# VectorE's order in the FFN down products: the fourth block sum behind two adds, the third sum beside the first, the last norm's tiles interleaved

## The reference, cut to what matters

```python
def conv_ffn(xn, w_up, conv_w, conv_b, w_down):      # w_up 1024 x 5632, w_down 2816 x 1024
    u = xn @ w_up
    up = jnp.pad(u, ((0, 0), (CONV_WIDTH - 1, 0), (0, 0)))
    c = conv_b
    for j in range(CONV_WIDTH):
        c = c + conv_w[j] * up[:, j:j + s]
    val, gate = jnp.split(c, 2, axis=-1)
    return (jax.nn.silu(gate) * val) @ w_down

for layer in range(2):
    h = h + merge_heads(heads) @ w_out[layer]
    h = h + conv_ffn(rmsnorm(h, norm_ffn[layer]), w_up[layer], ...)
return rmsnorm(h, norm_final)
```

## Time and profile before

| what | us |
|---|---|
| median of 3 runs | 1731.66 (1730.42 to 1731.68) |
| the profiled execution: its time | 1731.79 |
| the profiled execution: its span from first to last instruction | 1730.0 |
| TensorE busy | 1701.5 (98% of the span) |
| VectorE busy | 1082.1 (63%) |
| GpSimd busy | 838.4 (48%) |
| ScalarE busy | 757.4 (44%) |

### The profile page before, as it was taken

The page is one execution under the profiler, slowest core; times in us unless marked ns, Lnnn a source line. Parts: engine busy times, 40 slices in busy tenths (PEclk is TensorE's granted clock), DMA queues, the critical chain, the costliest instruction groups (busy, mean ns, idle before and its releaser), DMA issues.

```text
span 1730.0 us, 25076 instructions
## 1 busy us (share of the span) xinstructions
PE 1701.5 (98%) x9544; PEld 1379.8 (80%) x9548; DVE 1082.1 (63%) x2221; ACT 757.4 (44%) x1606; POOL 838.4 (48%) x784
## 2 busy tenths in 40 slices
PE   9999999999999999999999999999999999999997
PEld 7886787787689877779878878787777988788785
DVE  6997734785653356525684684757775368568477
ACT  4626523213433344424444444446663364345345
POOL 8525456552357734335535535266443554453440
PEclk9999999999999999999999999999999999999998
DMA  6321323131233311124225224132112241441521
GB/s 186 109 81 54 112 63 119 53 108 37 80 102 119 107 53 49 55 69 117 79 73 146 73 77 131 52 131 98 49 50 73 74 135 49 122 122 49 155 64 49
DMA packets 174600, 152.46 MB, mean 88 GB/s; under 512 B 5720, under 2 KB 149464, under 8 KB 174480
## 3 DMA queue, kind: packets, MB, share of 16 engines
q1 hardware_dynamic: 172304, 148.32, 27.9%
q10 hardware_dynamic: 2176, 2.53, 0.4%
HBM read 147.65 MB, written 2.14 MB: 87 GB/s over the span
## 4 chain that ended last, share of the span: by engine, by line
PE 83%; DVE 13%; ACT 3%; issue 1%; DVEq 0%; ACTq 0%
PE ps L490 66%; DVE ffn_cv L2890 2%; PE ps L2425 2%; PE ps L2460 2%; PE ps L2445 2%; DVE h L2742 2%; DVE w_lo L341 2%; DVE ffn_cv L2904 1%; PE ps L1892 1%; DVE ffn_a_lo L2911 1%; PE ps L561 1%; PE ps L1870 1%; PE ps L2433 1%; DVE w_chain L320 1%; PE ps L1807 1%
## 5 line engine op out<-in xcount | busy, mean ns | idle before, releaser
L490 PE MATMUL ps<-x_hi,w_hi 128*128 128x512 f32 (+2 forms) x1432 | 532.3, 372 | 0.5 <-DVE x_lo L762 0.4
L490 PE MATMUL ps<-x_hi,w_lo 128*128 128x512 f32 (+2 forms) x1432 | 522.6, 365 | 0.0
L490 PE MATMUL ps<-x_lo,w_hi 128*128 128x512 f32 (+2 forms) x1432 | 522.2, 365 | 0.0
L223 POOL TENSOR_SCALAR w_hi<-w_raw 128x512 fp32r<-128x512 f32 x272 | 167.8, 643 | 501.2 <-PE ps L490 501.2
L227 POOL TENSOR_TENSOR w_lo<-w_raw,w_hi 128x512 fp32r<-128x512 f32 x272 | 360.1, 1354 | 5.9
L195 POOL TENSOR_TENSOR w_lo<-w_raw,w_hi 128x512 fp32r<-128x512 f32 x174 | 232.9, 1372 | 267.8 <-ACT w_hi L186 235.4
L490 PEld LDWEIGHTS ps<-x_hi,w_hi 128*128 128x128 f32 (+1 forms) x1432 | 269.4, 188 | 60.0 <-issue 16.5
L490 PEld LDWEIGHTS ps<-x_hi,w_lo 128*128 128x128 f32 (+1 forms) x1432 | 269.3, 188 | 44.0
L490 PEld LDWEIGHTS ps<-x_lo,w_hi 128*128 128x128 f32 (+1 forms) x1432 | 269.7, 188 | 40.3
L2890 DVE SCALAR_TENSOR_TENSOR ffn_cv<-ps,col,ffn_cv 128x510 f32<-128x510 f32 (+1 forms) x176 | 131.8, 749 | 150.8 <-ACT ffn_cv L2836 146.2
L490 PE MATMUL ps<-w_hi,ffn_a_hi 128*128 128x512 f32 x308 | 122.7, 398 | 10.7 <-DVE h L2742 10.0
(11 more groups left out here) (396 smaller groups left out, 2873.2 us busy)
## 6 DMA issues: line engine op xcount, KB each, us to landing
w_raw<-w_up SPq DMA_DIRECT2D x88, 512.0 KB, 5.0
w_raw<-od_w_in SPq DMA_DIRECT2D x12, 1024.0 KB, 5.3
w_raw<-w_in_fox SPq DMA_DIRECT2D x10, 1024.0 KB, 5.4
w_raw<-w_in_dil SPq DMA_DIRECT2D x10, 1024.0 KB, 5.3
w_raw<-w_out SPq DMA_DIRECT2D x8, 1024.0 KB, 5.0
w_raw<-w_down SPq DMA_DIRECT2D x8, 1024.0 KB, 5.0
w_raw<-ev_w_in SPq DMA_DIRECT2D x6, 1024.0 KB, 5.4
w_third<-w_down SPq DMA_DIRECT2D x18, 256.0 KB, 5.2
```

The source lines that it names most:

```text
L223: ins = pool.tensor_scalar(hi[:, c:min(c + PIECE, size)], raw[:, c:min(c + PIECE, size)], 1.0, 1.0, ALU.mult, ALU.mult)
L490: mm = pe.matmul(o, l, r, start=start and i == 0, stop=stop and i == 2, skip_group_check=again)
```

## The change

Five edits, all in the order of instructions; none is added or removed but the semaphore counts that follow from the order.

1. `early`: the fourth sum moves from behind the low of 6 to behind X6 t1, just ahead of the low of 4.
2. `early`: X6 t0 is taken ahead of Z t1.
3. `ConvFFN.vector`: the third sum moves from behind the low of unit n-2 to directly behind the first sum, ahead of the conv of unit n-2.
4. The four takes of X7 and X7b become a function `sevens`, called at the same place as before, but in layer 1's last part from within `Final.vector`.
5. `Final`: VectorE's and ScalarE's instructions go tile by tile interleaved instead of tile behind tile.

```diff
-            READS = ("X1", "X1", "Y5", "Y5", "Z", "Z", "X6", "X6", "X7", "X7b", "X7", "X7b", "Y3", "Y3", "W", "W")
+            READS = ("X1", "X1", "Y5", "Y5", "Z", "X6", "Z", "X6", "X7", "X7b", "X7", "X7b", "Y3", "Y3", "W", "W")
@@ early
                 g.low(dve, "6")
-                g.fourth_sum(dve)
                 g.low(dve, "7")
                 self.take(dve, "Y5", 0, "5")
                 self.take(dve, "Y5", 1, "5")
                 self.take(dve, "Z", 0, "2")
+                self.take(dve, "X6", 0, "6")
                 self.take(dve, "Z", 1, "2")
-                self.take(dve, "X6", 0, "6")
                 g.low(dve, "3")
                 self.take(dve, "X6", 1, "6")
+                g.fourth_sum(dve)
                 g.low(dve, "4")
+
+            def sevens(self, dve):
+
                 for t in range(2):
                     self.take(dve, "X7", t, "7")
                     self.take(dve, "X7b", t, "7")
@@ ConvFFN.vector
                         if u == u0 + n - 2:
                             self.down[part].group.first_sum(dve)
+                            self.down[part].group.third_sum(dve)
                         conv(u)
                         gate(u)
                         a11, a21 = cv[:, u % 4, 0, 0:2 * P], cv[:, u % 4, 0, 2 * P:S]
                         low(u, 1, 0, 1, a11).then_inc(self.first_ready.s, 1)
                         if u == u0 + n - 2:
-                            self.down[part].group.third_sum(dve)
                             self.down[part].group.second_sum(dve)
...
                     d.early(dve)
+                    if part < len(PARTS) - 1 or self.layer == 0:
+                        d.sevens(dve)
@@ Final.scalar
+                for tile in range(T):
+                    first(tile)
+                for tile in range(2):
+                    root(tile)
+                    scaled(tile)
+                for tile in range(2, T):
+                    root(tile)
+                for tile in range(2, T):
+                    scaled(tile)
@@ Final.vector
+                dve.wait_ge(self.gain_in, 16)
+                first(0)
+                first(1)
+                self.out.sevens(dve)
+                first(2)
+                add(0)
+                first(3)
+                inverse(0)
+                add(1)
+                last(0)
+                inverse(1)
+                last(1)
+                add(2)
+                add(3)
+                inverse(2)
+                last(2)
+                inverse(3)
+                last(3)
```

More of the change, by code:

```diff
@@ L2671, in __init__, with taken @@
                 self.summed, self.read = tally("down_summed", 7), tally("down_read", 16)
-                self.added = self.Added(self.read)
+                self.added = self.Added(self)
+            def taken(self, what, t):
+                return self.read.at([i for i, r in enumerate(self.READS) if r == what][t] + 1)
             def sums(self, pe, m, c, t, js, start):
@@ L2706, in last_half @@
                 for t in range(2):
-                    pe.wait_ge(self.read.s, self.read.at(1 + t))
+                    pe.wait_ge(self.read.s, self.taken("X1", t))
                     self.sums(pe, "6", "X", t, every, False)
@@ L2710, in last_half @@
                 for t in range(2):
-                    pe.wait_ge(self.read.s, self.read.at(7 + t))
+                    pe.wait_ge(self.read.s, self.taken("X6", t))
                     self.sums(pe, "7", "X", t, every, False)
@@ L2717, in last_tile @@
                     pe.wait_ge(W.lo_by_dve, g.lows + 3)
-                    pe.wait_ge(self.read.s, self.read.at(3 + t))
+                    pe.wait_ge(self.read.s, self.taken("Y5", t))
                     self.sums(pe, "3", "Y", t, range(g.kk), False)
@@ L2737, in take @@
                 r, c = self.TARGET[what]
-                before = {"Z": 1, "X7b": 3, "Y3": 7, "W": 9}.get(what)
+                before = {"Z": "X1", "X7b": "Y5", "Y3": "X6", "W": "X7"}.get(what)
                 if before:
-                    dve.wait_ge(self.read.s, self.read.at(before + t * (2 if what == "W" else 1)))
+                    dve.wait_ge(self.read.s, self.taken(before, t))
                 hv = h[:, 2 * r + t, 512 * c:512 * c + 512]
@@ L2812, in up @@
                     d = self.down[part - 1]
-                    taken = {d.bank["X"]: 12, d.bank["Y"]: 14, d.bank["Z"]: 6, d.bank["W"]: 16}
-                    pe.wait_ge(d.read.s, d.read.at(taken[self.up_bank(u, 0)]))
+                    last = {d.bank[what[0]]: what for what in ("X7b", "Y3", "Z", "W")}
+                    pe.wait_ge(d.read.s, d.taken(last[self.up_bank(u, 0)], 1))
                 for half in range(2):
@@ L2977, in scalar, with first @@
                 link(act.activation(seam_stat[:, 0, 0:1], eps_col[:, 0:1], ACT.Sqrt))
-                for tile in range(T):
+                def first(tile):
                     act.wait_ge(self.out.added.s, self.out.added.at(tile + 1))
@@ L2981, in scalar, with root @@
                                    accum_out=seam_stat[:, 0, tile:tile + 1]).then_inc(self.first_summed, 1)
-                for tile in range(T):
+                def root(tile):
                     act.wait_ge(self.out.added.s, self.out.added.at(4 + tile + 1))
@@ L2988, in scalar, with scaled @@
                                    bias=self.first[:, tile:tile + 1]).then_inc(self.rooted.s, 1)
+                def scaled(tile):
                     act.wait_ge(self.inverted.s, self.inverted.at(tile + 1))
@@ L2993, in scalar, with first @@
                     act.dma_start(out[0, tile * P:(tile + 1) * P, self.early(tile)], self.res[:, tile, self.early(tile)]).then_inc(self.stored, 16)
+                for tile in range(T):
[7 more added lines that the diff above has]
+                    scaled(tile)
             def vector(self, dve):
-                dve.wait_ge(self.gain_in, 16)
-                for tile in range(T):
+                def first(tile):
                     e = self.early(tile)
@@ L3002, in vector, with inverse, last @@
                                       ALU.add).then_inc(self.first_made, 1)
-                for tile in range(T):
-                    e = self.late(tile)
-                    self.out.add(dve, 1, tile)
+                def inverse(tile):
                     dve.wait_ge(self.rooted.s, self.rooted.at(tile + 1))
                     dve.reciprocal(seam_stat[:, 2, tile:tile + 1], seam_stat[:, 1, tile:tile + 1]).then_inc(self.inverted.s, 1)
+                def last(tile):
+                    e = self.late(tile)
                     dve.wait_ge(self.inverted.s, self.inverted.at(tile + 1))
@@ L3010, in vector, with add @@
                                              self.gain[:, e], ALU.mult, ALU.mult).then_inc(self.last_ready, 1)
+                def add(tile):
+                    self.out.add(dve, 1, tile)
+                dve.wait_ge(self.gain_in, 16)
[16 more added lines that the diff above has]
+                last(3)
         memory = Memory((3, 7, 0, 1), (2, 4, 5, 6), od_out)
```

8 lines of the change are left out of this document (4 added, 4 removed).

## The result

The change made the kernel slower: 1749.40 us (median of 4 runs, 1748.37 to 1749.82) against 1731.09 (4 runs, 1730.42 to 1731.68), a ratio of 1.0104 with a 95% interval of 1.0091 to 1.0117. The forecast was 1743.0, range 1735 to 1750. So direction and range hold, and the point is 6.4 us short. The profiled execution took 1748.37 us, its span is 1746.6, 16.6 us longer than before.

A forecast was written before the change was run, and what follows sets the result against it. TensorE was busy 98% of the span, so time changes only where it waits and behind its last matmul. From 1731.79: +14.0 (3.5 in each of four kk-4 parts) - 1.6 - 1.1 = 1743.1, median 1743.0 us; range 1735 to 1750.

The forecast's parts named there:

- Edits 1 and 2, kk 4: Product 7, kk-4 parts: X6 t0 can come 3.0 us earlier; the 1.5 us gap and most of 0.2 go.
- Edit 3: Kk-4 parts: third sum delays the conv, `first_ready` falls at 878.05, and TensorE stalls 3.85 us at product 1.
- Turns with GpSimd: Third sum, kk 4: VectorE and GpSimd alternate instructions, so it takes 4 x 1.69 = 6.8 us, not 2.4.
- net term of 2.0 a part: Product 7 t1, kk-4 parts: starts at 902.6 instead of 900.4 with its 0.2, +2.0 us.
- The clock: Behind each kk-4 stall the granted clock falls, costing 1.5 us a part (bounds 0 and 3.4).
- The load behind the fourth sum: SyncE's first load waits for the later fourth sum; cover 0.3 us, costed at nothing, up to 1 us a part in the range.
- The late load: Rival: the load lands 0.3 us or more later than reckoned, each next part's first unit waits up to 1 us: 1747; chance 0.05.
- Third parts: Kk 3: third sum takes no turns; layer 0 gains 1.6 us, layer 1 gains 1.1 us (bounds 0 and -3.2).
- The new wait at 7 t1: Third parts, kk 3: X6 t1 ends at 1706.63, 7 t1 due at 1705.8; wait of 0.95 us, too short for the clock.
- no turns: Rival: third sum runs at 0.60 us an instruction beside GpSimd, no stall at product 1: 1721.4 us; chance 0.14.
- the clock not falling: Rival: clock stays up behind the new stall, or low stretch lies within it: 1737.0; chance 0.17, including part of it.

The follow-up runs named there:

- experiment 9: Kernel of experiment 8, with Y3 t0 taken ahead of the X7 takes in both third parts, takes split by tile in seam and last norm: 1715.11 us.
- experiment 2: Edit 3 alone on the kernel before (third sum directly behind the first): 1747.06 us, ratio 1.0092.
- experiment 4: Changed kernel with the fourth sum back behind the low of 6 (edit 1 undone, edits 2 to 5 kept): 1744.72 us, ratio 1.0079.
- experiment 1: Changed kernel with the third sum back behind the low of unit n-2 (edit 3 undone, all else kept): 1725.47 us, ratio 0.9965.
- experiment 3: Changed kernel, same order, with GpSimd's low of product 5 in eight 128x256 pieces instead of four 128x512: 1733.59 us, ratio 1.0013.
- experiment 7: Kernel of experiment 1, with the second load behind each group held until the first has landed: 1724.63 us, ratio 0.9962.
- experiment 8: Kernel of experiment 1 with `early` reordered: Y5 t0 ahead of low 7, X6 t0, fourth sum and X6 t1 ahead of Z's takes: 1721.69 us.
- experiment 5: Edits 1 and 2 alone on the kernel before, third sum and last norm as before: 1725.73 us, ratio 0.9972.

## Why the prediction was right, and where it fell short

**Edits 1 and 2, kk 4: right.** The gap at product 7 goes. In the run where only they are made (ahead of what the late load takes again), and in experiment 9, that is worth 1.8 to 1.9 us a part. That it is worth nothing once edit 3 is in the kernel (experiments 2 and 4) the prediction had built in, by judging product 7 from the stalled start.

**Edit 3: right in kind and in size.** Turns with GpSimd, 4 x 1.69 = 6.8 us predicted, 6.6 measured. `first_ready` at 878.05 predicted, at 877.99 in the trace; the stall 3.85 predicted, 3.83 to 3.85 measured; product 7 t0 at 899.9 predicted and at 899.98 measured, 7 t1 at 902.6 and at 902.70. Its net term of 2.0 a part was 2.16. The row that carried it, the earlier stage in the earlier trace rows, was of another line and another target, and still gave the right price; shape, operands and neighbour were alike. Experiments 1, 2 and 3 show it from three sides.

**The clock: the mean was near, the picture wrong.** Predicted 1.5 us in each of four parts, 6.0 in all. Measured 0.1, 1.7, 2.6 and 2.9, 7.3 in all. The bounds (0 and 3.4) held each of them. I had argued from one low stretch of 3.4 us, as behind the waits of 2.3 us, partly within the stall. In the trace there is none in part 1, one of 3.4 us wholly behind the stall in part 2, and two of 6.8 us in layer 1, of which 1.5 and 0.8 us fall within the stall. That they average near 1.5 is luck. What decides between them is open: the stall was the same in all four to 0.02 us, and in experiments 2 and 4, with the same stalls, the clock fell behind part 1's too.

**The load behind the fourth sum: this is the step that failed.** The prediction gave it 0.3 us of cover and cost nothing. Measured 4.0 us, 0.7 to 1.35 in each part. Two numbers of that step were off. It put the load's landing 5.1 us behind the fourth sum, from the earlier trace rows, where 5.0 is the median of single issues. But a load is two issues, the second 0.4 us behind the first, and has landed with the second. The page's DMA part for the second issue in the first part, before (from 892.45 to 892.6 us) and after (from 905.5 to 905.7):

```profile
w_raw<-w_up SPq DMA_DIRECT2D x1, 512.0 KB, 5.2
```

```profile
w_raw<-w_up SPq DMA_DIRECT2D x1, 512.0 KB, 5.6
```

From its first issue the whole load takes 5.6 us before and 6.0 after; in the other three parts 5.7 each before, and 6.6, 6.0 and 6.5 after. So half a microsecond was missing even for a load that goes alone. The rest has a cause in the same edit: the buffer of the second load comes free with the low of 3, some 8 us behind the fourth sum before, and ahead of it now, so that both loads go out at once. Experiment 7 puts the sharing itself at some 0.3 us in the first part. And GpSimd's split ended at 916.8 instead of 915.9, for which TensorE was due at 916.1 to 916.3. The trace of before had what was needed to foresee it: the row stands for both loads, the first issued at 891.99 and the second at 899.75 us, each in two issues. A cover of 0.3 us against a step of 11 us shouldn't have been costed at nothing. The late load was a case with a price of 4 us and a chance of 0.05; it was the likely one.

**Third parts: right, slightly more than predicted.** Layer 0 -1.6 predicted and measured. Layer 1 -1.1 predicted, -1.7 measured: TensorE's last matmul came 3.1 us earlier (3.2 predicted), and the tail gave 1.4 back where 2.1 were reckoned. The new wait at 7 t1 is there with 0.59 us, 0.95 with its ragged restart, and the clock doesn't fall behind it. The third sum took no turns with kk 3: on VectorE's timeline of after, layer 0,

```profile
1104.66 1.90 DVE L302 TENSOR_TENSOR w_third<-w_raw,w_third 128x512 f32<-128x512 f32 x3
```

which is 0.60 apart. The rows of the tail: `first` and the last store, which answer to the earlier trace rows:

```profile
1729.77 0.69 DVE L3023 TENSOR_TENSOR res<-h,final_gain 128x512 f32<-128x512 f32 x1 [1.23 <-ACT res L2990]
...
1743.80 0.34 ACTq L3006 DMA_DIRECT2D y<-res  x1
```

Product 7 t0 begins at 1722.07 there, so `first` 0 lies 7.7 us behind it (7.6 predicted, 7.2 before) and the last store 21.7 (about 22 predicted).

**The sum.** Against the profiled execution of 1748.37 us the forecast lacked 5.2: 4.0 for the loads, 1.3 for the clock, 0.65 for the stall's net, less 0.6 for the third parts. The rest, to the median, is that the profiled execution was the fastest of the four; its mean granted clock is 0.993, that of the others 0.991 and 0.992. The rivals: no turns (1721.4) is refuted by the spacing of 1.65 us and by experiment 3. What the change is worth without turns is experiment 1's 1725.5, since this rival left out the late loads (3.2 us there) and the clock's fall in the seam; that experiment 8 comes near 1721.4 is chance; the clock not falling is true of one part in four.

**What stays open.** Why the clock's loss differs between four equal stalls, and what of the load's lateness beyond the fourth sum's place is sharing in the kernel after itself (experiment 7 was made on the kernel of experiment 1, where the stall isn't), above all in the second parts, where the load took longest.

## What to carry to other kernels

Moving an instruction with two SBUF operands costs what its new neighbour on GpSimd makes of it: look for a stretch of the same trace in which these two engines run such instructions in rows side by side, and take the spacing from there; if the order must stay, cut GpSimd's pieces (15.8 of 18.3 us came back so). Follow every buffer that the moved instruction releases: the load behind it starts later, it has landed only with its last issue (5.6 to 5.7 us here, not the 5.0 of a single one), and if two loads start together it takes longer still (6.0 to 6.6). Two edits that end in the same tail need not add up (5.2 and 3.7 us apart, 5.8 together), and one that creates a stall upstream makes the repair downstream worthless: try them one at a time.

## What the runs showed of the hardware that I had not expected

Four stalls of 3.83 to 3.85 us at the same place of the program, in one execution, were followed by a granted clock of 1.00, 0.72, 0.57 and 0.50 over the next six microseconds, and cost 0.1 to 2.9 us beyond themselves. With the eight equal stalls of experiments 2 and 4 (3.82 to 3.85 us) the clock fell behind eleven of twelve, for 3.4 or 6.8 us. Stalls of 1.6 us at the same place (experiment 3) were followed by 1.00 in all four. And in the seam of layer 0 two waits for the normed tiles, 1.1 and 1.65 us with 1.1 us of work between them, were followed by a fall in the profiled executions of experiments 1, 5 and 7 (a granted clock of 0.72, 0.54 and 0.50 from 1136 to 1142 us), and by none in those of the kernel after and of experiment 3, where the six microseconds around and behind them show 1.00.

A turn lasts as long as the other engine's instruction: beside GpSimd's 128x512 subtractions VectorE's come 1.65 us apart, beside 128x256 ones 1.15, alone 0.60; and GpSimd, with twice the instructions for the same elements, was done in 7.54 us instead of 6.49 while VectorE was done sooner.
